# Fusing a final norm with the next mixer's norm, and starting attention scores before the value slab, in a float32 two-block transformer on one core

## What is computed

```
y  = rmsnorm(x, final_g)            # end of the first block, mean of squares over 1024 channels, eps 1e-6
xn = _rms(y, norm_mix[0])           # start of the second block
q, k, v for 16 heads of 64 = xn @ w_in_ab     # heads 0..7 "moba", heads 8..15 "dilated"
q, k normalised per head (rms over 64 channels, with gains), softmax(q k^T + bias) v
h = y + o @ w_out_ab                # y is needed again for the residual
```

## Time and profile before

| what | us |
|---|---|
| median of 3 runs | 2900.24 |
| lowest and highest | 2899.81, 2912.12 |
| the profiled execution's own time | 2900.88 |
| its span, first to last instruction | 2898.9 |
| PE busy, weight loads busy | 2687.6 (93%), 2263.1 (78%) |
| DVE busy, ACT busy | 1563.7 (54%), 1320.6 (46%) |
| mean granted TensorE clock | 0.953 |

### The profile page before, as it was taken

The page is one execution under the profiler, slowest core; times in us unless marked ns, Lnnn a source line. Parts: engine busy times, 40 slices in busy tenths (PEclk is TensorE's granted clock), DMA queues, the critical chain, the costliest instruction groups (busy, mean ns, idle before and its releaser), DMA issues. The chain is left out here.

```text
span 2898.9 us, 40646 instructions
## 1 busy us (share of the span) xinstructions
PE 2687.6 (93%) x15617; PEld 2263.1 (78%) x15617; DVE 1563.7 (54%) x2281; ACT 1320.6 (46%) x2001; POOL 22.0 (1%) x34
## 2 busy tenths in 40 slices
PE   6999998998899999899999798997899998889998
PEld 3788786875688877688876657997669997768998
DVE  7444434885644433644323565545757656556655
ACT  6444323464544422544312354544446544445644
POOL 0000000000000000000000000000000001000000
PEclk9999998999999999999999899999999999779999
DMA  6444532201344422344322202544215544302544
GB/s 244 174 159 163 191 138 73 97 20 44 119 170 153 165 102 101 122 168 155 131 90 100 103 1 81 181 174 162 102 59 188 181 178 162 128 11 73 188 174 145
DMA packets 52721, 374.81 MB, mean 129 GB/s; under 512 B 5823, under 2 KB 7035, under 8 KB 8737
## 3 DMA queue, kind: packets, MB, share of 16 engines
q1 hardware_dynamic: 50288, 360.73, 34.7%
q0 software_dynamic: 1920, 12.27, 1.2%
q10 hardware_dynamic: 432, 0.73, 0.1%
HBM read 372.55 MB, written 7.39 MB: 131 GB/s over the span
## 5 line engine op out<-in xcount | busy, mean ns | idle before, releaser
L1092 DVE TENSOR_TENSOR wlo<-raw,whi 128x1024 fp32r<-128x1024 f32 x666 | 799.6, 1222 | 823.0 <-ACT whi L657 821.9
L657 ACT ACTIVATE whi<-raw 128x1024 fp32r<-128x1024 f32 x666 | 684.7, 1053 | 867.6 <-PE acc L1586 781.5
L1584 PE MATMUL acc<-hhi,whi 128*128 128x256 f32 (+1 forms) x2800 | 939.7, 336 | 53.9 <-DVE hlo L1176 36.2
L1585 PE MATMUL acc<-hlo,whi 128*128 128x256 f32 (+1 forms) x2800 | 934.0, 334 | 0.0
L1586 PE MATMUL acc<-hhi,wlo 128*128 128x256 f32 (+1 forms) x2800 | 933.0, 333 | 0.0
L1584 PEld LDWEIGHTS acc<-hhi,whi 128*128 128x128 f32 x2800 | 536.4, 192 | 117.0 <-issue 61.9
L1586 PEld LDWEIGHTS acc<-hhi,wlo 128*128 128x128 f32 x2800 | 536.4, 192 | 50.8
L1585 PEld LDWEIGHTS acc<-hlo,whi 128*128 128x128 f32 x2800 | 536.8, 192 | 48.8 <-issue 0.2
L1584 PE MATMUL acc<-ghi,whi 128*128 128x512 f32 (+1 forms) x1056 | 364.0, 345 | 22.5 <-DVE glo L1249 15.1
L1585 PE MATMUL acc<-glo,whi 128*128 128x512 f32 (+1 forms) x1056 | 362.8, 344 | 0.0
L1586 PE MATMUL acc<-ghi,wlo 128*128 128x512 f32 (+1 forms) x1056 | 362.5, 343 | 0.0
(11 more groups left out here) (245 smaller groups left out, 2584.6 us busy)
## 6 DMA issues: line engine op xcount, KB each, us to landing
raw<-in_slabs SPq DMA_DIRECT2D x333, 1024.0 KB, 4.8
ada_raw<-in_slabs SPq DMA_DIRECT2D x8, 1024.0 KB, 22.8
skew_dram<-lines_dram POOLq DMA_DIRECT2D x1, 6144.0 KB, 24.9
bt<-skew_dram POOLq DMA_DIRECT2D x4, 1024.0 KB, 6.5
x<-in_x_in SPq DMA_DIRECT2D x1, 2048.0 KB, 18.0
out<-x SPq DMA_DIRECT2D x1, 1024.0 KB, 4.8
rope<-in_rope POOLq DMA_DIRECT2D x1, 512.0 KB, 4.0
mask<-in_mask POOLq DMA_DIRECT2D x1, 512.0 KB, 4.7
```

Source lines behind the costliest of these rows:

```text
L657: nc.scalar.activation(whi[:, n % 2, cols], raw_of(n, cols), ACT.Copy).then_inc(ready, 1)
L1092: nc.vector.tensor_tensor(wlo[:, n % 2, cols], raw_of(n, cols), whi[:, n % 2, cols].bitcast(F32), ALU.subtract).then_inc(low, 1)
L1584: nc.tensor.matmul(out, w[0], xx[0], start=first, stop=False)
L1585: nc.tensor.matmul(out, w[0], xx[1], start=False, stop=False)
```

## The change

Four edits that hang together, shown as a diff cut to its core.

The final norm has no stage of its own any more. The down stage before it (`both`) keeps two sums of squares, one of `x` times the root of eps and one of `x * final_g`, in 2 by 512 columns of `prod`; the mixer's norm takes its root from their total, with the product of the two gains; a second root, from the first sum alone, is left in the upper half of `rs` for later.

The final scaling of `x` itself is done by DVE among the units of att: a reciprocal after unit 11 and one tile after each of the units 12 to 19.

The head norms of slabs 6 and 7 leave qknorm; DVE does them in four pieces of one tile after units 3, 5, 7 and 9.

PE no longer waits for `att_ready`; the scores of units 0, 1 and 2 come ahead of the first value slab, with waits of their own.

```diff
-    st += [Stage("norm", T=S, how="final")]
+    st[-1].both = True
     for layer in range(2):
         st += [Stage("norm", T=S, how="gain", gain=VCOL["norm_mix"] + DT * layer)]
+        st[-1].both = layer == 0
...
 @ pool, norm_share, and dve, norm
                 pool.wait_ge(rs_ready, st.rs0 + 1)
+                if st.both:
+                    pool.wait_ge(x_summed, 1)
...
 @ act, root
+                nc.scalar.activation(rs[:, 0:st.T], sums[:, 0:st.T], ACT.Sqrt,
+                                     bias=(eps_sq if st.both else eps)[:, 0:1], scale=1.0 / D).then_inc(std_ready, 1)
+                if st.both:
+                    act.wait_ge(x_summed, 1)
+                    nc.scalar.activation(rs[:, S:2 * S], B[2][:, 0:S], ACT.Sqrt, bias=eps[:, 0:1],
+                                         scale=1.0 / (D * ROOT_EPS * ROOT_EPS)).then_inc(x_root, 1)
...
 @ act, residual
-                                nc.scalar.activation(sq[:, :, 0:st.T], x[:, bass.ds(2 * c + 4 * i, 2), 0:st.T],
-                                                     ACT.Square).then_inc(sq_ready, 1)
+                                ins = nc.scalar.activation(sq[:, :, 0:st.T], x[:, bass.ds(2 * c + 4 * i, 2), 0:st.T],
+                                                           ACT.Square, scale=ROOT_EPS if st.both else 1.0)
+                                for t in range(2) if st.both else ():
+                                    g = VCOL["final_g"] + 2 * c + t + 4 * i
+                                    ins = nc.scalar.activation(sq[:, t, S:2 * S], x[:, 2 * c + t + 4 * i, 0:S],
+                                                               ACT.Square, scale=vec[:, g:g + 1])
+                                ins.then_inc(sq_ready, 1)
...
-                if st.feeds:
+                if st.feeds or st.both:
                     half(0)
                     half(1)
...
-                if st.feeds:
+                if st.feeds or st.both:
                     preload(ACT.Sqrt)
...
 @ dve, residual: wide = 2 * S if st.both
-                                nc.vector.tensor_tensor(prod[:, :, 0:st.T], prod[:, :, 0:st.T], sq[:, :, 0:st.T],
+                                nc.vector.tensor_tensor(prod[:, :, 0:wide], prod[:, :, 0:wide], sq[:, :, 0:wide],
                                                         ALU.add).then_inc(sq_added, 1)
...
 @ pe, added_sums
+                if st.both:
+                    for c in range(2):
+                        nc.tensor.matmul(sums[:, 0:S], ones, prod[:, c, S:2 * S], start=(c == 0), stop=False)
+                    for c in range(2):
+                        ins = nc.tensor.matmul(sums[:, 0:S], ones, prod[:, c, 0:S], start=False,
+                                               stop=(c == 1))
+                    ins.then_inc(sum_done, 1)
+                    for c in range(2):
+                        ins = nc.tensor.matmul(B[2][:, 0:S], ones, prod[:, c, 0:S], start=(c == 0), stop=(c == 1))
+                    ins.then_inc(x_summed, 1)
+                    return
...
 @ dve, qknorm: the loop runs one round less for 8 slabs
+                if st.slabs == 8:
+                    lo(n + 8)
+                    lo(n + 9)
+
+            def late_head_norm(i):
+
+                st = [s for s in plan if s.kind == "qknorm" and s.slabs == 8][0]
+                c, cols = i // 2, slice(S * (i % 2), S * (i % 2) + S)
+                dve.wait_ge(std_ready, st.std0 + c + 7)
+                step.done(nc.vector.reciprocal(prod[:, c, cols], prod[:, c, cols]))
+                g = st.gain + 6 + c
+                step.done(nc.vector.scalar_tensor_tensor(QK[:, 12 + i, :], QK[:, 12 + i, :], vec[:, g:g + 1],
+                                                         prod[:, c, cols], ALU.mult, ALU.mult))
+                if i % 2:
+                    nc.vector.memset(junk[:, :], 0.0).then_inc(qk_done, 1)
...
 @ dve, att, after biased(u + LEAD)
+                    if st.what == "ab" and u == 11:
+                        dve.wait_ge(x_root, 1)
+                        step.done(nc.vector.reciprocal(rs[:, S:2 * S], rs[:, S:2 * S]))
+                    if st.what == "ab" and 12 <= u < 20:
+                        c, g = u - 12, VCOL["final_g"] + u - 12
+                        step.done(nc.vector.scalar_tensor_tensor(x[:, c, 0:S], x[:, c, 0:S], vec[:, g:g + 1],
+                                                                 rs[:, S:2 * S], ALU.mult, ALU.mult))
+                    if st.what == "ab" and u in (3, 5, 7, 9):
+                        late_head_norm(u // 2 - 1)
...
 @ pe, att
-                pe.wait_ge(att_ready, st.att0 + 1)
                 if st.what != "ab":
+                    pe.wait_ge(att_ready, st.att0 + 1)
...
-                if ab:
-                    for step in range(16):
-                        value_step(0, step)
-
                 def scores(u):
...
+                    if ab and u % 8 == 0:
+                        pe.wait_ge(qk_done, 2 + st.qk0 - 3 + u // 8)
+                    if ab and u == 1:
+                        pe.wait_ge(std_ready, st.std0)
...
                 for u in range(LEAD):
                     scores(u)
+                if ab:
+                    for step in range(16):
+                        value_step(0, step)
```

More of the change, by code:

```diff
@@ L134, in __init__ @@
         self.ada, self.gate, self.how, self.gain, self.what = ada, gate, how, gain, what
-        self.late, self.feeds, self.norm = False, None, None
+        self.late, self.feeds, self.norm, self.both = False, None, None, False
 def ffn_stages(layer, tokens, ada=0, mod=None):
@@ L429, in build @@
         ple_added = sem("ple_added")
+        x_summed = sem("x_summed")
+        x_root = sem("x_root")
         silu_done = sem("silu_done")
@@ L521, in turn_bank, with gain_of @@
             return acc[:, 1, 1, :] if st.what == "ab" else acc[:, u % 2, 1, :]
+        def gain_of(st, c):
+            return two_gains[:, c:c + 1] if st.both else vec[:, st.gain + c:st.gain + c + 1]
         def scaled_row(engine, st, k):
@@ L528, in scaled_row @@
                 g = mA[:, st.mod, c, s:s + 1]
-            elif st.how == "gain":
-                g = vec[:, st.gain + c:st.gain + c + 1]
-            else:
-                g = vec[:, VCOL["final_g"] + c:VCOL["final_g"] + c + 1]
-            dst = x[:, c, cols] if st.how == "final" else ub[:, k % 4, :]
+            else:
+                g = gain_of(st, c)
+            dst = ub[:, k % 4, :]
             return engine.scalar_tensor_tensor(dst, x[:, c, cols], g, rs[:, cols], ALU.mult, ALU.mult)
@@ L567, in _ @@
             nc.gpsimd.memset(arow[:, :, :], 0.0).then_inc(eps_ready, 1)
+            nc.gpsimd.memset(eps_sq[:, :], EPS * EPS).then_inc(eps_ready, 1)
             pool.sem_inc(acc_free[0], 1)
@@ L692, in root @@
                 act.wait_ge(sum_done, st.sum0 + (1 if st.summed else DT))
-                nc.scalar.activation(rs[:, 0:st.T], sums[:, 0:st.T], ACT.Sqrt, bias=eps[:, 0:1], scale=1.0 / D)\
-                    .then_inc(std_ready, 1)
+                nc.scalar.activation(rs[:, 0:st.T], sums[:, 0:st.T], ACT.Sqrt,
[4 more added lines that the diff above has]
+                                         scale=1.0 / (D * ROOT_EPS * ROOT_EPS)).then_inc(x_root, 1)
             def ada(st):
@@ L798, in norm @@
                     root(st)
-                if st.how == "final":
-                    return
                 for k in range(st.items):
@@ L813, in norm @@
                     elif k % 2:
-                        ins = nc.scalar.activation(dst, ub[:, k % 4, :], ACT.Copy,
-                                                   scale=vec[:, st.gain + c:st.gain + c + 1])
+                        ins = nc.scalar.activation(dst, ub[:, k % 4, :], ACT.Copy, scale=gain_of(st, c))
                     else:
@@ L1112, in start @@
                     nc.vector.tensor_scalar(vec[:, col:col + 4], vec[:, col:col + 4], HD ** -0.5, None, ALU.mult)
+                f, g = VCOL["final_g"], VCOL["norm_mix"]
+                step.done(nc.vector.tensor_tensor(two_gains[:, :], vec[:, f:f + DT], vec[:, g:g + DT], ALU.mult))
             def inverse(st):
@@ L1166, in norm @@
                 dve.wait_ge(rs_ready, st.rs0 + 1)
+                if st.both:
+                    dve.wait_ge(x_summed, 1)
                 def scaled(k):
@@ L1179, in low @@
                     elif k % 2:
-                        g = st.gain + c
-                        ins = nc.vector.scalar_tensor_tensor(hlo[:, c, cols], ub[:, k % 4, :], vec[:, g:g + 1],
+                        ins = nc.vector.scalar_tensor_tensor(hlo[:, c, cols], ub[:, k % 4, :], gain_of(st, c),
                                                              hhi[:, c, cols].bitcast(F32), ALU.mult, ALU.subtract)
@@ L1186, in low @@
                     ins.then_inc(h_ready, 1)
-                if st.how == "final":
-                    for k in range(st.items):
-                        scaled(k)
-                    return
```

(10 more changed lines are left out.)

9 lines of the change are left out of this document (6 added, 3 removed).

## The result

| kernel | median, us | lowest to highest | runs |
|---|---|---|---|
| before | 2901.16 | 2899.81 to 2913.23 | 9 |
| after | 2921.98 | 2919.97 to 2927.27 | 9 |

The ratio is 1.0058, with a 95% interval of 1.0035 to 1.0081. The kernel became slower; 2887.2 was forecast, and the range ended at 2895. The runs of the kernel before lie in two groups, five from 2899.81 to 2901.16 and four from 2910.25 to 2913.23, and the kernel after is slower than both. The profiled execution took 2922.24 (span 2920.2, mean granted clock 0.937; before 2898.9 and 0.953).

A forecast was written before the change was run, and what follows sets the result against it. PE was taken to bound nearly every stage except the norm and last head-norm stretches. Norm -11.2, att -1.9 (-9.6 + 7.7) and start +0.1 summed to -13.0 us, so 2887.2 against the median 2900.24; range 2882 to 2895.

The forecast's parts named there:

- the clock in att: Attention stage: PE's clock stays at 1.00 in spite of existing 0.47 us waits, so no cost in the main forecast.
- the sum: Whole kernel: norm part -11.2, att -1.9 and start +0.1 give -13.0 us, so 2887.2.
- rival 4: Att: clock falls to half at unit 4's wait, 20 units at 1.4 us more, 28 in all; 2907.5, chance 0.05.
- signs of being wrong: PE waiting for a slab in down, clock 0.5 in units 4 to 20, or transposes not waiting at units 4 and 12.
- Norm: Last residual to mixer's first scaled row: one fused chain with the table load hidden gains 11.2 us.
- Down: Down stage: each group's extra 1 us on ACT and 0.53 on DVE is covered, nothing lost; at most 3 x 0.5.
- Start of att: Att's start: new PE wait of 1.5 us, only DVE's 0.9 really hidden, first exponential earlier by 9.6 us.
- Late pieces: DVE's moved head norms and x scaling among att's units make PE wait, giving back 7.7 us.
- Rival 1: Att: DVE's idle time swallows the late work, so the 7.7 us comes back; 2879.5, chance 0.10.
- Rival 2: Norm sums and mixer: PE starts both warm, saving 0.5 and about 1.5 us; 2885.2, chance 0.13.
- Rival 3: Att: no slack, each late piece delays the next unit in full, 15.0 us instead of 7.7; 2894.5, chance 0.13.
- The table load: Norm part: root's 1.28 us load is hidden, no second cost; the skill page's 1.38 drain would give some 2888.5.

The follow-up runs named there:

- run 7: Changed kernel with the first value slab ahead of the scores again, late head norms and fused norm kept; 2913.61 us, ratio 1.0016.
- run 5: Changed kernel with exponentials ahead of value-row copies, x scaled before qknorm's first round, late head norms recut and moved into DVE's idle time; 2876.28 us, ratio 0.9904.
- run 9: run 5 with the final norm and mixer norm as two separate steps, as in the kernel before; 2900.91 us, ratio 0.9998.
- run 4: Changed kernel with ACT's exponentials of units 0 to 2 ahead of its copies of the value rows; 2907.45 us, ratio 1.0006.
- run 2: Changed kernel with the two norms of before, keeping late head norms and scores first; 2935.14 us, four runs at 2896.67 to 2898.44, six at 2935.09 to 2937.7.
- run 8: Changed kernel with 36 thrown-away matmuls in a row after unit 15; 2908.29 us.
- run 1: Changed kernel with only the fused norm and x scaled among the units; head norms and order of scores and slab as before; 2929.49 us, ratio 1.0062.
- run 6: Kernel before with 8 thrown-away matmuls added ahead of the first value slab; 2942.49 us, ratio 1.012.
- run 10: run 5 with 24 thrown-away matmuls ahead of unit 0 in the window attention and the second layer's; 2873.23 us, ratio 0.99.
- run 11: Second profile of the unchanged kernel of run 9; 2901.96 us.

## Why the prediction was wrong

**The step that failed is the clock in att, which the sum put at 1.00 and so at no cost**, and left to rival 4. The clock was priced only where PE stood still for long: 0.5 us, of at most 0.9, at the sums of squares. What the runs show in its place is 0.50 for 116 us, 41.2 us in the sum. For att the prediction said that the clock "has 1.00 now in spite of its 0.47 waits" and gave the fall 0.05. Two things were wrong with that:
- It looked at the 0.47 and not at unit 0's own wait of 2.15, which stands in the trace of before and is the one that matters. With two falls in 27 runs of the kernel before and four in four with the wait 0.37 us later, a clock of 1.00 in one profile was no evidence that a wait is harmless. It was one draw.
- It tied the fall to the new waits from unit 4 on. The fall came at unit 0, in a wait that the sum did not count as changed: 2.39 us instead of 2.15, and 19.7 us earlier. By run 7 the new waits can lose the clock too.

The mechanism of rival 4 was right, its size too small: 1.4 us a unit and 20 units were priced, 28 in all; 1.65 and all 24 units with a value slab, and the last ones at half rate too, are 41.2. The ratio of 1.6 was taken from another attention; in these units it is 287 to 170, 1.69. Rival 4's 2907.5 is 14.5 below the median, 13.2 of it for that reason and 1.0 for the norm. Two of the prediction's own signs of being wrong are in the profile: a clock of 0.50 in units 4 to 20, and transposes that don't wait at units 4 and 12.

**What the other steps said, against the trace:**
- *Norm.* 11.2 forecast, 10.2 in the profile, 9.7 to 11.0 between runs 5 and 9. DVE's sum of squares starts 0.3 earlier than thought (1992.67); all four sums of PE run at half rate (2.08 and 1.91, against 1.13), not the last two. The root waits 1.81 for PE; the table load is hidden.
- *Down.* PE is busy 40.00 of 40 at 1.00: no wait for a slab, as forecast.
- *Start of att.* The new wait is 1.59 (forecast 1.5); the first exponential comes 9.5 earlier than the norm explains (9.6). The copies of the value rows and the table load are not hidden, as the prediction says.
- *Late pieces.* 2.15, 1.01, 0.22, 0.83, 1.01 and 1.63 in run 4 up to its fall: 6.85, and 6.4 less the 0.47 that was there before, against 6.7 in the sum for these places. The other 1.0 of the 7.7 (units 14 and 19) lies behind the fall. In the kernel after they cost nothing, because PE at half rate gives DVE time: the one such wait left is 0.45. The cost that was forecast vanished, and a larger one stood in its place.
- *Rival 1* (DVE's idle time swallows the work) is what run 5 makes true by placing the pieces: 2876.28 against its 2879.5. *Rival 2*: the sums ran at half rate, so no. *Rival 3*: no, by run 4.

With the clock kept, the change would probably have been near its forecast. Run 2's four warm runs lie at 2896.67 to 2898.44; with 10 to 11 us off for the fused norm and the sum's 2.7 on for the reciprocal and the products of `x`, an estimate is 2888 to 2891, 1 to 4 above the forecast and inside its range. No run shows this kernel with the clock kept.

**The table load.** The prediction put no second cost behind a table load. That stands: 1994.55 + 1.28, and the next instruction starts at 1995.84.

## What to carry to other kernels

Where TensorE works in small bursts, price every wait of a microsecond or two at what the rest of the loop costs at half the clock, also an old wait that is only moved, and look at several runs of the kernel before for executions that have already lost the clock. Cut moved work into pieces that fit each unit's measured slack, rather than trusting the total of idle time. When a change makes a kernel slower though its idle stretches got shorter, compare the number of matmuls and the granted clock per stretch, not the busy share.

## What the runs showed of the hardware

- Once low, the unit loop stays low though PE is busy; at full clock it stays there as long as its waits are short (0.48 us at most in 62 us of run 5). PE is busy 52.00 of 52 us at 0.50 with 170 matmuls, and 50.58 of 52 at 1.00 with 287. At 0.50 it stayed for up to 116 us; what brought it back in these runs was dense work: wo's slabs, 36 matmuls in a row (run 8), and ahead of the units the first value slab (before: from its start at 2080.96 to 2084.0).
- Waits of 1.6 to 2.4 us were enough to lose it, and the same wait was survived in some executions and not in others of one kernel (run 2, 2.39 us: 4 and 6; before, 2.15 us: 25 and 2 of 27). The same wait of 2.15 us was lost in 5 of 5 when it came 10.4 us earlier (run 1) and in 4 of 4 when it came 0.37 us later (run 6). So the length of the wait alone does not decide; whether its time does or what PE did before it, these runs do not separate, and the rule behind it is open. "TensorE: Matmul & The Clock Gate" in the Trainium skill, section "Why this matters for your kernels", warns against idle gaps between bursts. The trace agrees that such gaps cost, with 38 us between run 2's two groups, but here gaps shorter than those that the page warns of were enough.
- In the last units, which have no value matmuls, the six profiles that reach them at full clock (before and runs 5, 8, 9, 10 and 11) all lose it within 2.4 us of the end of the same wait of 1.02 us (1.01 in run 11); run 4 keeps it over two waits of 1.01 us among units that have them.
- The second layer's attention has a lottery of its own, over when the clock comes back. It is low there from 2487.1 in run 9 and 2490.2 in run 11, so from before the wait of 4.17 us, and stays so for 81.9 and for 99.0 us; that costs 7.7 us.
